# Attention loop: copy, turn, sums and scaling of finished heads placed in other periods

## The chip, the cores and the metric

One core of one Trainium2 chip runs the whole program. The metric is the device time of one launch in microseconds. The engines are TensorE (PE), its weight loads (PEld), VectorE (DVE), ScalarE (ACT), GpSimd (POOL) and SyncE (SP), which issues the DMAs.

## The reference

Two layers of an encoder on 1024 tokens of width 1024 in float32, which lie on a grid of 16 rows by 64 columns. Each layer mixes the tokens in three groups of heads (8 heads of neighbourhood attention, 4 of spatial gating, 4 of a Fourier mix), norms every head, projects, and then applies a SwiGLU network:

```python
for l in range(DEPTH):
    proj = rms_norm(x, norm_mix_g[l]) @ w_in[l]
    q, k, v, z_b, x_c = jnp.split(proj, splits, axis=-1)
    mix_a = neighbourhood_attention(q, k, v, rpb[l])
    mix_b = spatial_gating(z_b, ...)
    mix_c = fourier_mix(x_c)
    mix = head_rms_norm(jnp.concatenate([mix_a, mix_b, mix_c], axis=-1), head_norm_g[l])
    x = x + mix @ w_out[l]
    h = rms_norm(x, norm_ffn_g[l])
    x = x + (jax.nn.silu(h @ w_gate[l]) * (h @ w_up[l])) @ w_down[l]
return rms_norm(x, final_norm_g)
```

In the attention every query sees a window of 8 rows by 16 columns of keys: `softmax(q k^T * scale + bias) v` per head. `head_rms_norm` divides each head's 64 values of a token by the root of their mean square.

## The kernel before, in words

Each engine has its own queue, written out by hand as one Python function per engine (`_(pe)`, `_(dve)`, `_(act)`, `_(pool)`, `_(sp)`), and the engines meet only in semaphores. The order in a queue is the order in which the helpers are called. Products in float32 precision are made of three passes over parts called hi and lo.

The attention of a layer works on eight tiles of 128 queries (`TILES`), each with 264 to 384 keys, and on eight heads per tile, so there are 64 score blocks, t = 8 * tile + head. They go in pairs i = t // 2. From pair 8 on, two pairs make a **period** m (pairs 2m and 2m+1, scores of heads 4m to 4m+3), m = 4 to 15; a tile is two periods, and it begins with an even one. Tiles 2 and 5 (m = 4, 5, 10, 11) have 352 keys, tiles 3 and 4 (m = 6 to 9) have 384, tile 6 has 264 and tile 7 has 288.

For one score block: `scores` (TensorE, L2382), `logits` (VectorE adds the bias and takes the maximum, L1760), `probs` (ScalarE's exponential, with its sum, L1185), `turn_halves` (TensorE turns the probabilities, L2538), `turned_even` and `turned_odd` (the probability copies out of the bank by VectorE, L1797, and ScalarE, L1210), `values` (TensorE multiplies with the values of two heads, L2457, into bank 6). `values` of period m are pairs 2m-2 and 2m-1: the last pair of a tile comes in the even period behind it.

The finished heads of a tile then pass these steps:

- `heads_copy` (VectorE, L1812): copy of bank 6; waits for the tile's last values. The next tile's first values wait for it.
- `turn_heads` (TensorE, L2472): turns them to token-major form in bank 7; waits for the copy and for `tile_raw` of the tile before, which frees the bank.
- `head_square` (ScalarE, L1223).
- `head_sums` (VectorE, L1784): the sums of 64 squares.
- add and power (GpSimd, L875 and L877): the reciprocal root. Ahead of the add stands the square of the exponential sums of the same tile (L872).
- `head_norms` (VectorE, L1817): the scaling, from bank 7 into the place of the squares.
- `turn_tokens` (TensorE, L2479): the turn back into bank 7; waits for the scaling.
- `tile_raw` (ScalarE, L1229): the raw copy of bank 7 into the mixed output.

GpSimd's queue also splits the pieces of the output weights (`piece_lo`, L821): one behind the power of tile 1, two behind that of tile 5, two behind that of tile 6. `probs` of the first head of a tile waits, from the third tile on, for the squared sums (L872) of the tile two before:

```python
if t >= 16 and t % 8 == 0:
    act.wait_ge(o_eps, l * 8 + t // 8 - 1)
```

Behind the loop, `out_early(0)` (three pieces of three passes, L2233 to L2235) begins the output projection; each piece waits for its `piece_lo`. Then come the last turns, heads 6 and 7, and the rest of the projection.

Of the kernel before, what the change touches and what calls it, by code (L numbers as in the profile page):

```python
# [186 lines left out]
def build(nc, x, win, wout, wom, wg, wu, wd, bias, wsp, bsp, lng, lnb, gmix, ghead, gffn, gfin,  # L187
          tw, bd, ident, out):
    ctx = ExitStack()
    with ctx:  # L190
# [317 lines left out]
        def keys(tile):  # L508
            j, rr = TILES[tile]
            return KR[rr] * KC[j]  # L510
# [387 lines left out]
        def _(act):  # L898
# [158 lines left out]
            for l in range(DEPTH):  # L1057
# [122 lines left out]
                def probs(t):  # L1180
                    act.wait_ge(l_made, l * 64 + t + 1)
                    if t >= 16 and t % 8 == 0:
                        act.wait_ge(o_eps, l * 8 + t // 8 - 1)
                    w = keys(t // 8)
                    nc.scalar.activation(L[:, t % 4, 0:w], L[:, t % 4, 0:w], ACT.Exp, scale=-1.0,  # L1185
                                         bias=NM[:, t % 4:t % 4 + 1],
                                         accum_out=SUM[:, (t // 8) % 2, t % 8:t % 8 + 1]).then_inc(p_made, 1)
# [13 lines left out]
                def turned_odd(t):  # L1201
                    act.wait_ge(pt_full, l * 64 + t + 1)
                    if t >= 4:
                        act.wait_ge(pv_done, l * 64 + t - 3)
                    w = chunk_keys(t // 8, 0)
                    if t < 2 * SINGLE:
                        nc.scalar.activation(head_probs(t)[0:w], B[3][0:w, 0:NKEY].rearrange("p (n q) -> p n q", q=P),
                                             ACT.Copy).then_inc(pt_act, 1)
                    else:
                        nc.scalar.activation(half_probs(t // 2, 1)[0:w],  # L1210
                                             B[3][0:w, 0:NKEY].rearrange("p (g q) -> p g q", q=DH),
                                             ACT.Copy).then_inc(pt_act, 1)
# [8 lines left out]
                def head_square(tile):  # L1221
                    act.wait_ge(o_turned, l * 8 + tile + 1)
                    nc.scalar.activation(head_squares(tile),  # L1223
                                         B[TILE_BANK[tile]][:, :].rearrange("p (k q) -> p k q", q=P), ACT.Square,
                                         scale=(DH * EPS) ** -0.5).then_inc(o_sq, 1)

                def tile_raw(tile):
                    act.wait_ge(ot_full, l * 8 + tile + 1)
                    nc.scalar.activation(raw_out(tile),  # L1229
                                         B[TILE_BANK[tile]][:, :].rearrange("p (k r c) -> p k r c", k=NP, c=QC),  # L1230
                                         ACT.Copy).then_inc(raw_made, 1)
# [12 lines left out]
                    for n in {0: (), 1: (0, 1, 2), 7: ()}.get(i, (i + 1,)):  # L1244
                        batch_hi(n)
                for m in range(SINGLE // 2, 16):
                    if m % 2 == 0 and m >= 6:
                        tile_raw((m - 6) // 2)
                    for n in {7: (0,), 15: (2,)}.get(m, ()):
                        piece_hi(l, OUT_P + n)  # L1250
                    probs(4 * m)
                    turned_odd(4 * m - 1)
                    probs(4 * m + 1)
                    if m % 2 == 0 and m >= 4:
                        head_square((m - 4) // 2)
                    probs(4 * m + 2)
                    probs(4 * m + 3)
                    if m == 14:
                        piece_hi(l, OUT_P + 1)
                    turned_odd(4 * m + 1)  # L1260
                tile_raw(5)
                turned_odd(63)
                head_square(6)
# [104 lines left out]
        def _(dve):  # L1368
# [136 lines left out]
            for l in range(DEPTH):  # L1505
# [244 lines left out]
                def logits(t):  # L1750

                    tile, h = divmod(t, 8)
                    dve.wait_ge(s_full, l * 64 + t + 1)
                    if t >= 4:
                        dve.wait_ge(pt_full, l * 64 + turns_done(t - 4))
                    if h % 4 == 0:
                        dve.wait_ge(bias_landed[BIAS_BUF[tile]][h // 4], l * 48 + 16 * BIAS_NTH[tile])
                    dve.sem_inc(dve_passed, 1)

                    nc.vector.tensor_tensor_reduce(  # L1760
                        L[:, t % 4, 0:keys(tile)], score_bank(t // 2, t % 2),
                        BIAS[BIAS_BUF[tile]][:, h // 4, h % 4 * keys(tile):(h % 4 + 1) * keys(tile)], -1.0, 3e38,
                        ALU.add, ALU.min, NM[:, t % 4:t % 4 + 1]).then_inc(l_made, 1)
# [13 lines left out]
                def head_sums(tile):  # L1777

                    dve.wait_ge(o_sq, l * 8 + tile + 1)
                    if tile:  # L1780
                        dve.wait_ge(o_rstd, l * 8 + tile)
                    else:
                        dve.wait_ge(hs_norm, l * 3 + 3)
                    nc.vector.tensor_reduce(SS[:, 0:HA].rearrange("p (k r) -> p k r", k=NP),  # L1784
                                            head_squares(tile).rearrange("p k (r d) -> p k r d", d=DH),
                                            AX_X, ALU.add).then_inc(o_red, 1)

                def turned_even(t):
                    dve.wait_ge(pt_full, l * 64 + t + 1)
                    if t >= 4:  # L1790
                        dve.wait_ge(pv_done, l * 64 + t - 3 + (t >= 2 * SINGLE))
                    w = chunk_keys(t // 8, 0)
                    if t < 2 * SINGLE:
                        nc.vector.tensor_copy(head_probs(t)[0:w], B[2][0:w, 0:NKEY].rearrange("p (n q) -> p n q", q=P))\
                            .then_inc(pt_dve, 1)
                    else:
                        nc.vector.tensor_copy(half_probs(t // 2, 0)[0:w],  # L1797
                                              B[2][0:w, 0:NKEY].rearrange("p (g q) -> p g q", q=DH)).then_inc(pt_dve, 1)
# [9 lines left out]
                def heads_copy(tile):  # L1808
                    dve.wait_ge(pv_done, l * 64 + 8 * tile + 8)
                    if tile:  # L1810
                        dve.wait_ge(o_turned, l * 8 + tile)
                    nc.vector.tensor_copy(OC[:, :, :], B[VALUE_BANK][:, :].rearrange("p (k q) -> p k q", q=P))\  # L1812
                        .then_inc(o_copied, 1)

                def head_norms(tile):
                    dve.wait_ge(o_rstd, l * 8 + tile + 1)
                    nc.vector.scalar_tensor_tensor(  # L1817
                        out=head_squares(tile).rearrange("p k (r d) -> p k r d", d=DH),
                        in0=B[TILE_BANK[tile]][:, :].rearrange("p (k r d) -> p k r d", k=NP, d=DH),
                        scalar=EPS ** -0.5,  # L1820
                        in1=SR[:, 0:HA].rearrange("p (k r a) -> p k r a", k=NP, a=1).to_broadcast([P, NP, 2, DH]),
                        op0=ALU.mult, op1=ALU.mult).then_inc(o_norm, 1)
# [13 lines left out]
                    if 2 <= i < 6:  # L1836
                        query_rest(0, i - 2)
                for m in range(SINGLE // 2, 16):
                    if m % 2:
                        heads_copy((m - 3) // 2)  # L1840
                    logits(4 * m)
                    logits(4 * m + 1)
                    turned_even(4 * m - 2)
                    if m % 2:
                        head_norms((m - 5) // 2)
                    logits(4 * m + 2)
                    logits(4 * m + 3)
                    if m % 2 == 0:
                        head_sums((m - 4) // 2)
                    turned_even(4 * m)  # L1850
                turned_even(62)
                head_sums(6)
                head_norms(6)
# [353 lines left out]
        def _(pe):  # L2207
# [29 lines left out]
            for l in range(DEPTH):  # L2237
# [33 lines left out]
                for i, (k, h) in enumerate(X_ORDER):  # L2271
# [7 lines left out]
                    for b in range(4 * h, 4 * h + 4):  # L2279
                        m = slice(b * P, (b + 1) * P)  # L2280
# [278 lines left out]
                for m in range(SINGLE // 2, 16):  # L2559
                    scores(2 * m)  # L2560
                    scores(2 * m + 1)
                    if 2 * m - 1 < SINGLE:
                        turn_pair(2 * m - 1)
                    else:
                        turn_halves(2 * m - 1)
                    if m % 2 == 0:
                        turn_heads((m - 4) // 2)
                    values(2 * m - 2)
                    values(2 * m - 1)
                    if m % 2:  # L2570
                        turn_tokens((m - 5) // 2)
                    turn_halves(2 * m)
                pe.wait_ge(bt_lo, l * 8 + 8)
                out_early(0)
                turn_halves(31)
                turn_heads(6)
                out_early(1)
# [250 lines left out]
```

## Time and profile before

| | |
|---|---|
| three runs | 2023.27, 2024.71, 2027.75 us (median 2024.71) |
| the profiled execution | 2022.06 us, its span 2020.0 us |
| TensorE busy | 1985.4 us, 98% of the span |
| VectorE, ScalarE, GpSimd busy | 1522.2, 895.4, 217.7 us |
| attention loop (m = 4 to 15) | layer 0: 229.69 to 283.87 us; layer 1: 1226.43 to 1280.60 us |
| TensorE's granted clock | 0.998 of full speed in the mean |

Matmuls are pipelined and the ends of their rows are modelled, so that rows of TensorE overlap; their starts say more than their durations. Idle time is printed in brackets with the engine that ended it; "issue" is time for which nothing is shown. A line of the timeline can stand for several like instructions (x12).

### The profile page before, as it was taken

To read this page: it belongs to the slowest core of one execution; us is meant where nothing else is said; L and a number is where in the kernel's file an instruction comes from. 1 tells how busy PE (TensorE), PEld (TensorE's weight loads), DVE (VectorE), ACT (ScalarE), POOL (GpSimd) and SP (SyncE) were. 2 spreads that over 40 slices of the span, in tenths; PEclk is the share of its full clock that TensorE was granted. 3 is DMA by queue.
4 is the path that set the end of the run, shared out by engine and by line. 5 is a ranking of instruction groups with operands and counts; after the bars stand their busy time and mean duration, and the time that the engine had idled before them with its cause. 6 is when DMAs were issued, how large, how long until landed. Compare 5 with 4: busy or idle time off the path is not lost.

```text
span 2020.0 us, 28668 instructions
## 1 busy us (share of the span) xinstructions
PE 1985.4 (98%) x10444; PEld 1651.2 (82%) x10444; DVE 1522.2 (75%) x2517; ACT 895.4 (44%) x1611; POOL 217.7 (11%) x150
## 2 busy tenths in 40 slices
PE   7999999999999999999999999999999999999998
PEld 7888778888888888888898877788888888888887
DVE  7847864798877777787877478557987777778877
ACT  6453873443333333544544548634333333334443
POOL 1221343100000000000013122530000000000000
PEclk9999999999999999999999999999999999999999
DMA  6965744125333337533378667431343333393333
GB/s 239 219 167 143 219 132 149 48 84 177 131 104 105 105 105 276 182 98 97 117 209 201 159 158 231 148 104 42 130 161 111 105 105 104 105 337 96 100 96 123
DMA packets 130986, 288.88 MB, mean 143 GB/s; under 512 B 12960, under 2 KB 17952, under 8 KB 130592
## 3 DMA queue, kind: packets, MB, share of 16 engines
q1 hardware_dynamic: 105184, 237.78, 36.1%
q0 software_dynamic: 10880, 20.97, 6.2%
q10 hardware_dynamic: 14784, 28.31, 3.9%
q8 instruction: 84, 1.38, 0.3%
q14 instruction: 54, 0.44, 0.1%
HBM read 227.77 MB, written 59.24 MB: 142 GB/s over the span
## 4 chain that ended last, share of the span: by engine, by line
PE 87%; DVE 6%; ACT 3%; issue 3%; ACTq 0%; POOL 0%; DMA 0%; DVEq 0%
PE bank L2233 27%; PE bank L2234 27%; PE bank L2235 27%; PE bank L2457 1%; PE bank L2382 1%; ACT logits L1185 1%; DVE s_lo L1474 1%; PE bank L2538 1%; DVE t_lo L1897 0%; DVE logits L1760 0%; PE bank L2479 0%; PE bank L2345 0%; ACT probs_t L1210 0%; ACT h_hi L915 0%; PE bank L2361 0%
## 5 line engine op out<-in xcount | busy, mean ns | idle before, releaser
L2233 PE MATMUL bank<-t_hi,s_hi 128*128 128x512 f32 (+1 forms) x1336 | 516.9, 387 | 0.7 <-DVE hid_cu L2010 0.4
L2234 PE MATMUL bank<-t_lo,s_hi 128*128 128x512 f32 (+1 forms) x1336 | 516.4, 386 | 0.0
L2235 PE MATMUL bank<-t_hi,s_lo 128*128 128x512 f32 (+1 forms) x1336 | 516.3, 386 | 0.0
L2233 PEld LDWEIGHTS bank<-t_hi,s_hi 128*128 128x128 f32 x1336 | 250.9, 188 | 52.5 <-DVE hid_cu L2010 1.3
L2235 PEld LDWEIGHTS bank<-t_hi,s_lo 128*128 128x128 f32 x1336 | 250.9, 188 | 50.9
L2234 PEld LDWEIGHTS bank<-t_lo,s_hi 128*128 128x128 f32 x1336 | 250.9, 188 | 50.6
L2233 PE MATMUL bank<-b_hi,s_hi 128*128 128x512 f32 x528 | 206.0, 390 | 0.1
L2235 PE MATMUL bank<-b_hi,s_lo 128*128 128x512 f32 x528 | 205.5, 389 | 0.0
L2234 PE MATMUL bank<-b_lo,s_hi 128*128 128x512 f32 x528 | 205.4, 389 | 0.0
L988 ACT ACTIVATE s_hi<-w_u 128x512 fp32r<-128x512 f32 x142 | 89.6, 631 | 232.7 <-PE bank L2235 175.2
L988 ACT ACTIVATE s_hi<-w_down 128x512 fp32r<-128x512 f32 x154 | 97.3, 632 | 198.7 <-PE bank L2235 198.0
L1474 DVE TENSOR_TENSOR s_lo<-w_down,s_hi 128x512 fp32r<-128x512 f32 x154 | 107.4, 698 | 74.0 <-ACT s_hi L988 73.9
L988 ACT ACTIVATE s_hi<-w_g 128x512 fp32r<-128x512 f32 x142 | 89.4, 630 | 162.9 <-PE bank L2235 104.9
L821 POOL TENSOR_TENSOR w_lo<-w_raw,w_hi 128x1024 fp32r<-128x1024 f32 x34 | 84.3, 2493 | 689.1 <-ACT w_hi L928 577.4
L928 ACT ACTIVATE w_hi<-w_raw 128x1024 fp32r<-128x1024 f32 x91 | 93.0, 1053 | 65.9 <-DMA w_raw<-in_win 47.9
L2233 PEld LDWEIGHTS bank<-b_hi,s_hi 128*128 128x128 f32 x528 | 99.1, 188 | 21.4 <-issue 0.9
L2235 PEld LDWEIGHTS bank<-b_hi,s_lo 128*128 128x128 f32 x528 | 99.1, 188 | 20.5
L2234 PEld LDWEIGHTS bank<-b_lo,s_hi 128*128 128x128 f32 x528 | 99.1, 188 | 20.4
L1484 DVE TENSOR_TENSOR t_lo<-t_raw,t_hi 128x512 fp32r<-128x512 f32 x154 | 105.4, 684 | 9.6 <-ACT t_hi L994 9.6
L1474 DVE TENSOR_TENSOR s_lo<-w_g,s_hi 128x512 fp32r<-128x512 f32 x142 | 97.3, 686 | 10.7 <-ACT s_hi L988 10.7
L2233 PE MATMUL bank<-h_hi,w_hi 128*128 128x512 f32 x256 | 101.1, 395 | 0.0
L994 ACT ACTIVATE t_hi<-t_raw 128x512 fp32r<-128x512 f32 x154 | 95.0, 617 | 12.8 <-DMA t_raw<-hidden_b 11.3
(295 smaller groups left out, 3705.8 us busy)
## 6 DMA issues: line engine op xcount, KB each, us to landing
w_raw<-in_win SPq DMA_DIRECT2D x50, 512.0 KB, 5.9
w_g<-in_wg SPq DMA_DIRECT2D x44, 512.0 KB, 3.6
w_u<-in_wu SPq DMA_DIRECT2D x44, 512.0 KB, 4.5
t_raw<-hidden_t SPq DMA_DIRECT2D x88, 256.0 KB, 2.6
w_raw<-in_win POOLq DMA_DIRECT2D x40, 512.0 KB, 6.7
t_raw<-hidden_b SPq DMA_DIRECT2D x66, 256.0 KB, 2.6
hidden_b<-hid_g SPq DMA_DIRECT2D x60, 256.0 KB, 2.0
hidden_t<-hid_x SPq DMA_DIRECT2D x44, 256.0 KB, 2.0
```

The source lines that it names most:

```text
L821: nc.gpsimd.tensor_tensor(WL[s][:, :], WR[s][:, :], WH[s][:, :], ALU.subtract).then_inc(w_ready, 1)
L928: nc.scalar.activation(WH[s][:, :], WR[s][:, :], ACT.Copy).then_inc(w_hi, 1)
L988: nc.scalar.activation(SH[q % W_RING][:, :], weight_block(q), ACT.Copy).then_inc(s_hi, 1)
L994: nc.scalar.activation(TH[t][:, :], TR[t][:, :], ACT.Copy).then_inc(t_hi, 1)
L1185: nc.scalar.activation(L[:, t % 4, 0:w], L[:, t % 4, 0:w], ACT.Exp, scale=-1.0, bias=NM[:, t % 4:t % 4 + 1], accum_out=SUM[:, (t // 8) % 2 ...
L1474: nc.vector.tensor_tensor(SL[q % W_RING][:, :], weight_block(q), SH[q % W_RING][:, :], ALU.subtract)\
L1484: nc.vector.tensor_tensor(TL[t][:, :], TR[t][:, :], TH[t][:, :], ALU.subtract).then_inc(t_lo, 1)
L2233: nc.tensor.matmul(bank, lh, rh, start=start, stop=False, skip_group_check=reopened)
L2234: nc.tensor.matmul(bank, lh, rl, start=False, stop=False, skip_group_check=reopened)
L2235: return nc.tensor.matmul(bank, ll, rh, start=False, stop=stop, skip_group_check=reopened)
L2382: mm = nc.tensor.matmul(score_bank(i, e).rearrange("p (r c) -> p r c", c=KC[j]), qs[hp, c, q0:q0 + P], grid(ks[hp, c, :])[:, 4 * rr:4 * rr ...
L2457: mm = nc.tensor.matmul(B[VALUE_BANK][e * DH:(e + 1) * DH, c * P:(c + 1) * P], VB[j % 2][0:w, rr + n, h * DH:(h + 1) * DH], head_probs(h, ...
```

## The change

Five calls change places, in the loops over m of three queues. Even periods: VectorE scales (tile (m-6)/2) behind the second logits, and copies the heads of the tile just finished at the end, instead of at the start of the odd period; TensorE turns back ahead of the values and turns the heads behind them; ScalarE makes the raw copy behind its second exponential and squares at the end. Odd periods: VectorE makes the sums behind its probability copy. What is left over of tile 5 moves behind the loop. In period 14 `piece_hi` stands behind `turned_odd`.

```diff
@@ ScalarE
                 for m in range(SINGLE // 2, 16):
-                    if m % 2 == 0 and m >= 6:
-                        tile_raw((m - 6) // 2)
                     for n in {7: (0,), 15: (2,)}.get(m, ()):
                         piece_hi(l, OUT_P + n)
                     probs(4 * m)
                     turned_odd(4 * m - 1)
                     probs(4 * m + 1)
-                    if m % 2 == 0 and m >= 4:
-                        head_square((m - 4) // 2)
+                    if m % 2 == 0 and m >= 6:
+                        tile_raw((m - 6) // 2)
                     probs(4 * m + 2)
                     probs(4 * m + 3)
+                    if m % 2 == 0:
+                        head_square((m - 4) // 2)
+                    turned_odd(4 * m + 1)
                     if m == 14:
                         piece_hi(l, OUT_P + 1)
-                    turned_odd(4 * m + 1)
@@ VectorE
                 for m in range(SINGLE // 2, 16):
-                    if m % 2:
-                        heads_copy((m - 3) // 2)
                     logits(4 * m)
                     logits(4 * m + 1)
+                    if m % 2 == 0 and m >= 6:
+                        head_norms((m - 6) // 2)
                     turned_even(4 * m - 2)
                     if m % 2:
-                        head_norms((m - 5) // 2)
+                        head_sums((m - 5) // 2)
                     logits(4 * m + 2)
                     logits(4 * m + 3)
                     if m % 2 == 0:
-                        head_sums((m - 4) // 2)
+                        heads_copy((m - 2) // 2)
                     turned_even(4 * m)
+                head_norms(5)
                 turned_even(62)
@@ TensorE
+                    if m % 2 == 0 and m >= 6:
+                        turn_tokens((m - 6) // 2)
+                    values(2 * m - 2)
+                    values(2 * m - 1)
                     if m % 2 == 0:
                         turn_heads((m - 4) // 2)
-                    values(2 * m - 2)
-                    values(2 * m - 1)
-                    if m % 2:
-                        turn_tokens((m - 5) // 2)
                     turn_halves(2 * m)
                 pe.wait_ge(bt_lo, l * 8 + 8)
                 out_early(0)
+                turn_tokens(5)
                 turn_halves(31)
```

TensorE's queue from the second scores of period 8 to the second turn of period 9, first before, then with the change (L2382, L2538 and so on are L2383, L2539 there, since a line is added above; of the six score rows of a period the last stands here). `att_sq` is turned back, `att_heads` turned.

```order
L2382 MATMUL bank<-k_hi,q_lo 128x384 x2
L2538 MATMUL bank<-ident,logits 128x64 x12
L2472 MATMUL bank<-ident,att_heads 128x128 x4
L2457 MATMUL bank<-probs_t,v_band_90 64x128 x12
L2538 MATMUL bank<-ident,logits 128x64 x12
...
L2538 MATMUL bank<-ident,logits 128x64 x12
L2457 MATMUL bank<-probs_t,v_band_89 64x128 x12
L2479 MATMUL bank<-ident,att_sq 128x128 x4
L2538 MATMUL bank<-ident,logits 128x64 x12
```

```order
L2383 MATMUL bank<-k_hi,q_lo 128x384 x2
L2539 MATMUL bank<-ident,logits 128x64 x12
L2480 MATMUL bank<-ident,att_sq 128x128 x4
L2458 MATMUL bank<-probs_t,v_band_90 64x128 x12
L2473 MATMUL bank<-ident,att_heads 128x128 x4
L2539 MATMUL bank<-ident,logits 128x64 x12
...
L2539 MATMUL bank<-ident,logits 128x64 x12
L2458 MATMUL bank<-probs_t,v_band_89 64x128 x12
L2539 MATMUL bank<-ident,logits 128x64 x12
```

The turn back has gone from the end of the odd period to the front of the values of the even one, and the turning of the heads from ahead of these values to behind them.

VectorE's queue over the even period 8 and the first rows of period 9, before and with the change. `att_heads` is the copy, `head_ss` the sums, `att_sq<-bank,head_rstd` the scaling.

```order
L1760 ISA logits,minus_max<-bank,bias_64 128x384
L1760 ISA minus_max 128x1
L1797 COPY probs_t<-bank 128x6x64
...
L1784 TENSOR_REDUCE head_ss<-att_sq 128x8
L1797 COPY probs_t<-bank 128x6x64
L1812 COPY att_heads<-bank 128x512
L1760 ISA logits,minus_max<-bank,bias_64 128x384
```

```order
L1760 ISA logits,minus_max<-bank,bias_64 128x384
L1760 ISA minus_max 128x1
L1817 SCALAR_TENSOR_TENSOR att_sq<-bank,head_rstd 128x4x128
L1797 COPY probs_t<-bank 128x6x64
...
L1812 COPY att_heads<-bank 128x512
L1797 COPY probs_t<-bank 128x6x64
L1760 ISA logits,minus_max<-bank,bias_64 128x384
```

The scaling stands between the second logits and the probability copy; the copy of the heads is the last but one of the even period; the sums have left it.

## Rows read from the trace of the kernel before

**Rows 1.** Table by stretches: start:end, us, busy us of each engine, PEclk, DMA share, GB/s
```profile
core 0: us, PE busy (x) PEld busy (x) DVE busy (x) ACT busy (x) POOL busy (x), PEclk, DMA share, GB/s
200.00:300.00 100.00, 92.12 (x1086) 74.37 (x1085) 75.11 (x207) 76.52 (x199) 37.73 (x32) 1.00 0.60 182
300.00:400.00 100.00, 100.00 (x464) 83.29 (x463) 60.43 (x81) 41.77 (x63) 29.58 (x13) 1.00 0.29 98
```
**Rows 2.** Timeline of TensorE, periods 8 and 9: start us, duration us, instruction
```profile
247.97 0.43 PE L2382 MATMUL bank<-k_hi,q_hi 64*128 64x384 f32 x2
...
249.14 0.53 PE L2538 MATMUL bank<-ident,logits 64*128 64x64 f32 x12
249.60 0.66 PE L2472 MATMUL bank<-ident,att_heads 128*128 128x128 f32 x4
250.18 1.53 PE L2457 MATMUL bank<-probs_t,v_band 128*64 128x128 f32 x24
251.64 0.59 PE L2538 MATMUL bank<-ident,logits 64*128 64x64 f32 x12
252.04 0.43 PE L2382 MATMUL bank<-k_hi,q_hi 64*128 64x384 f32 x2
...
255.26 0.88 PE L2457 MATMUL bank<-probs_t,v_band 128*64 128x128 f32 x12 [0.45 <-ACT probs_t L1210]
256.06 0.66 PE L2479 MATMUL bank<-ident,att_sq 128*128 128x128 f32 x4
...
257.05 0.41 PE L2382 MATMUL bank<-k_hi,q_hi 64*128 64x352 f32 x2
```
**Rows 3.** Timeline of VectorE, periods 8 and 9, and one row of period 15
```profile
248.97 0.56 DVE L1760 CUSTOM_DVE_ANT_0 logits<-bank,bias 128x384 f32<-128x384 f32 x1 [0.22 <-PE bank L2382]
...
249.94 0.55 DVE L1797 COPY probs_t<-bank 128x384 f32<-128x384 f32 x1
...
251.77 0.69 DVE L1784 TENSOR_REDUCE head_ss<-att_sq 128x8 f32<-128x512 f32 x1 [0.33 <-ACT att_sq L1223]
...
252.84 0.68 DVE L1812 COPY att_heads<-bank 128x512 f32<-128x512 f32 x1
253.44 0.55 DVE L1760 CUSTOM_DVE_ANT_0 logits<-bank,bias 128x384 f32<-128x384 f32 x1
...
254.86 0.68 DVE L1817 SCALAR_TENSOR_TENSOR att_sq<-bank,head_rstd 128x512 f32<-128x512 f32 x1
...
279.73 0.45 DVE L1760 CUSTOM_DVE_ANT_0 logits<-bank,bias 128x288 f32<-128x288 f32 x1
```
**Rows 4.** Timeline of ScalarE, period 8, and its probability copy in period 9
```profile
248.62 0.59 ACT L1229 ACTIVATE att_raw<-bank 128x512 f32<-128x512 f32 x1
249.58 0.61 ACT L1185 ACTIVATE logits<-logits,minus_max 128x384 f32<-128x384 f32 x1 [0.36 <-DVE minus_max L1760]
...
250.19 0.47 ACT L1210 ACTIVATE probs_t<-bank 128x384 f32<-128x384 f32 x1
250.56 0.60 ACT L1185 ACTIVATE logits<-logits,minus_max 128x384 f32<-128x384 f32 x1
...
254.64 0.47 ACT L1210 ACTIVATE probs_t<-bank 128x384 f32<-128x384 f32 x1
```
**Rows 5.** Timeline of GpSimd: the power in period 9, the two pieces in period 15
```profile
252.88 1.64 POOL L877 TENSOR_TENSOR head_rstd<-head_ss,minus_half 128x8 f32<-128x8 f32 x1
...
280.40 4.70 POOL L821 TENSOR_TENSOR w_lo<-w_raw,w_hi 128x1024 fp32r<-128x1024 f32 x2
```
**Rows 6.** Timeline of TensorE: start of period 15, first early product, last turns
```profile
278.05 0.38 PE L2382 MATMUL bank<-k_hi,q_hi 64*128 64x288 f32 x2
...
283.87 0.50 PE L2233 MATMUL bank<-h_hi,w_hi 128*128 128x512 f32 x1
...
286.14 0.54 PE L2538 MATMUL bank<-ident,logits 64*96 64x64 f32 x12
286.61 0.66 PE L2472 MATMUL bank<-ident,att_heads 128*128 128x128 f32 x4
```
**Rows 7.** Table by stretches, columns as in rows 1, two microseconds near the end
```profile
2014.00:2016.00 2.00, 0.40 (x2) 0.11 (x1) 1.56 (x4) 0.00 (x0) 0.00 (x0) 0.50 0.80 263
```

## The prediction

> **What bounds the kernel now.** I read the table by stretches first. TensorE is busy for all of 300 to 400 us but for only 92.12 us of 200 to 300 us [rows 1]: the attention stage is where TensorE waits, and the stage behind it has no gap in which a later start could be made up. So what lengthens or shortens TensorE's attention loop goes to the end one for one. Both layers run the same program, so each term counts twice.
>
> Next the timeline of TensorE over one even and one odd period (m = 8 and 9, 384 keys) [rows 2]. Even, from 247.97 (called T): scores, probabilities turned at T+1.17, heads turned at T+1.63, values at T+2.21, probabilities turned at T+3.67, next period at T+4.07. Odd, from 252.04 (T'): the second head pair's values begin only at T'+3.22, after an idle time that ScalarE's probability copy ended; turn back at T'+4.02, next period at T'+5.01. The two cost 9.08 us. VectorE shows why the odd one is late: it copies the heads at 252.84, ahead of the logits, the first of which thus begins at T'+1.40, where in the even period it begins at T+1.00 [rows 3].
>
> **The even period afterwards.** The turn back now stands ahead of the values and waits for the scaling, which VectorE does behind the first two logits. These cannot begin before T+1.00, since they need this period's scores (the row's idle time is ended by them). The scaling takes the place of the probability copy that began at 249.94, T+1.97, and lasts 0.68 us [rows 3]: done at T+2.65. From a producer's end to TensorE's start I take 0.15 us: ScalarE's probability copy that begins at 254.64 ends at 255.11 [rows 4], and TensorE's values, which waited for it, begin at 255.26 [rows 2]. TensorE has nothing to do from T+1.63 on and stands for about 1.15 us, until T+2.80. From there all is back to back with the pitches of rows 2: turn back 0.59, values 1.46, heads turned 0.58, probabilities turned 0.40: next period at T+5.83. Two waits could be longer and are not. The turning of the heads needs the raw copy of the tile before: ScalarE can start it at T+3.46 (end of the turn back, 0.66 us), its second exponential having begun at T+2.59, and needs 0.59 us [rows 4]; done by T+4.1, needed at T+4.85. The copy of the heads waits for the last values (T+4.9) with the next probability copy queued behind it on VectorE, but that one needs a turn that ends at T+6.0 anyway. An even period goes from 4.07 to 5.83 us, **+1.76**. There are five with a turn back (m = 6, 8, ... 14): +8.8.
>
> **The odd period afterwards.** Copy of heads, scaling and turn back are gone; the sums are added behind the probability copy. The logits begin at T'+1.00 again, so the exponential and ScalarE's probability copy stand as in the even rows: the copy begins at T'+2.22 and lasts 0.47 [rows 4], the second values begin at T'+2.84, take 0.73 (half of 1.46), the turn 0.40: next period at T'+3.97 against 5.01, **-1.04**. The sums (0.69 us) delay only the last two logits, whose exponentials are wanted in the following period at about T+1.2, ahead of its new wait. Five such periods (m = 5, 7, ... 13): -5.2. The first even period (m = 4) only turns the heads behind the values instead of ahead of them: between 0 and 0.58, and 0.1 taken, because the values then wait for ScalarE's probability copy (T+2.84, and they begin at T+2.21 now).
>
> **GpSimd, which the diff does not touch.** Its queue is in program order: add and power per tile, behind tile 1 one piece of the output weights to split, behind tile 5 two, and only then the squared exponential sums of the next tile. The power (1.64 us) begins 0.42 us after the end of the sums (251.77 and 0.69 [rows 3], 252.88 [rows 5]); two pieces take 4.70 us [rows 5]. All of it hangs on the sums, which move from the end of the even period to T'+2.43 of the odd one (1.97 and a copy's pitch of 0.46).
> - Tile 1 (m = 7): sums end at T'+3.1, power 3.5 to 5.2, piece to 7.5, squared sums there at 7.6. The next period begins at 3.97, so this is T+3.65 of m = 8, and ScalarE's first exponential of that tile, which waits for them, began at T+1.61 until now [rows 4]. Behind it the probability copy ends at T+4.8, second values at 4.95, second exponential 4.7, raw copy 5.3 to 5.9, heads turned 5.95, next period at T+6.93: **+1.1** on top of the 1.76.
> - Tile 5 (m = 15, T' = 278.05): today the pieces run from 280.40 to 285.10, T'+7.05 [rows 5], and the early output products, three pieces of 0.76 us each, begin at 283.87, T'+5.82 [rows 6], so that the last piece is just in time. Now the sums end at about T'+2.8 (288 keys: logits of 0.45 instead of 0.55 us [rows 3] and shorter scores, 0.3 less than above), power 3.2 to 4.85, pieces to 7.15 and 9.5. TensorE comes to the products between T'+4 and T'+5, wherever ScalarE lets it, does one, and stands until 7.25 for the second piece and until 9.6 for the third; it is through at T'+10.35 instead of 8.09 (286.14). Then the turn back of tile 5, new at this place, and its raw copy (0.66, 0.59 and 0.1 between) stand ahead of the turning of heads 6: T'+11.7 instead of 8.56 (286.61) [rows 6]: **+3.14**. The later steps of the tail (powers of tiles 6 and 7, more pieces) I cost at nothing: they move by no more than TensorE does, with the early products as cover; without that cover each would cost up to the 2.35 us of a piece.
>
> **Sum.** 8.8 - 5.2 + 0.1 + 1.1 + 3.14 = 7.9 us per layer; for the four tiles of fewer keys, with shorter logits ahead of the new wait, I take off 0.4. 7.5 us twice is 15.0. The profiled execution took 2022.06 us (span 2020.0), which gives 2037.1; the three runs shown have their median at 2024.71, 2.65 above it, and against that I forecast **2039.7 us**, +0.74%. A measurement of this kernel can tell about 0.2% (4 us) from no change.
>
> **A rule against it.** The attention stretch keeps the granted clock at 1.00 with 8 us of idle in it [rows 1]; at the very end, with TensorE busy for 0.40 of 2 us, it is 0.50, which is 1.2 GHz [rows 7]. The change makes two stands of about 1.5 us close together in the early products; whether the clock falls there is a rival below. The Trainium skill, "TensorE: Matmul & The Clock Gate", Part 1, says that an idle array is put on half clock and gets the full one back by activity; by that rule the sum would grow by that rival's price, by the clock in rows 1 it does not.
>
> **The rivals.**
> - *Only TensorE's wait costs.* If the squared sums and the pieces come in time, 1.1 goes, and the 3.14 becomes about 0 (-1.0 in period 15 as in the other odd ones, +0.6 and +0.3 for turn back and raw copy behind the products): 3.3 per layer, 2031.3. For it: no such wait is in the rows today. Against: GpSimd's order and 2.35 us a piece. Chance 0.14.
> - *Faster.* The place is the turn back in the even period, and the end of the scaling decides. If TensorE finds it done at T+1.63, that period is 4.07 + 0.59 = 4.66 and the pair 8.63 instead of 9.08: -0.45 for each of five tiles, and with GpSimd hidden too 2.3 per layer, 2020.1 in all. For it: the late logits of the odd periods do go. Against: VectorE would have to take logits before their scores are there. Chance 0.05.
> - *No change that shows.* The waits come out half as long as I have them, because the edges are smoother than the pitches of two periods say: 2024.7 give or take 4. Chance 0.06.
> - *The clock falls* in the stands of the tail: the early products, 2.27 us at full clock [rows 6], take double, and at most as much again is lost behind them: 2.3 to 4.5 per layer, 2044 to 2049. Chance 0.07.
> - The forecast case keeps 0.68.
>
> **How the numbers follow.** Around the forecast, 0.2 us either way on five even periods and 0.5 on the tail are 1.5 per layer, 3 in all, and the median of a few runs moves by some 2: 2035 to 2045. To leave out no more than 2 in 10 the range takes in the first rival and the lower half of the clock's: 2030.5 to 2047. Faster by over 0.2%: 0.05; within it: 0.06; slower: 0.89.
>
> **What the profile of the changed kernel would show.** A turn back at T+2.8 in even periods, with 1.1 us of idle ended by VectorE's scaling; even periods of 5.8 us (6.9 for m = 8), odd ones of 4.0; GpSimd's two pieces ending near T'+9.5 of period 15, and two stands of 1.5 us inside the first early products. I am wrong if even periods stay below 5 us, if the early products run without a gap, or if TensorE is no longer full from 300 to 400 us.

## The result, and the profile after

The changed kernel takes 2043.18 us in the median of 6 runs (2040.97 to 2043.76), the kernel before 2028.03 us in the 6 runs on the same chips (2023.27 to 2029.96). The ratio is 1.008 with a 95% interval of 1.0069 to 1.0091: 0.8% slower, 14 to 18 us. The profiled execution took 2040.97 us, its span is 2039.0 us against 2020.0.

The forecast was 2039.7 us, +0.74%, against a median of 2024.71 us for the kernel before; the three further runs took 2028.31 to 2029.96 and raised it to 2028.03. The last section shows what the granted clock has to do with that.

The table by stretches first (columns as in [rows 1]); the last two rows are the tail of the attention in layer 1:

```profile
core 0: us, PE busy (x) PEld busy (x) DVE busy (x) ACT busy (x) POOL busy (x), PEclk, DMA share, GB/s
200.00:300.00 100.00, 85.80 (x1047) 67.49 (x1046) 72.36 (x202) 73.50 (x193) 32.27 (x28) 1.00 0.59 178
300.00:400.00 100.00, 100.00 (x467) 83.30 (x466) 57.67 (x77) 40.01 (x60) 34.95 (x18) 1.00 0.31 100
1295.00:1300.00 5.00, 3.07 (x10) 2.19 (x10) 0.00 (x0) 0.00 (x0) 3.00 (x3) 0.72 0.49 196
1300.00:1305.00 5.00, 5.00 (x27) 3.80 (x25) 1.24 (x2) 3.57 (x5) 1.16 (x2) 0.59 0.01 2
```

TensorE is now busy for 85.80 us of the attention stretch instead of 92.12 [rows 1], and still for all of the next one: what is lost is lost in the attention and is not made up. The next rows are TensorE's timeline over an even and an odd period of 384 keys (m = 6 from 238.35, m = 7 from 244.10), the changed kernel's answer to [rows 2]:

```profile
238.35 0.43 PE L2383 MATMUL bank<-k_hi,q_hi 64*128 64x384 f32 x2
...
239.63 0.57 PE L2539 MATMUL bank<-ident,logits 64*128 64x64 f32 x12
241.06 0.65 PE L2480 MATMUL bank<-ident,att_sq 128*128 128x128 f32 x4 [0.85 <-DVE att_sq L1817]
241.64 1.54 PE L2458 MATMUL bank<-probs_t,v_band 128*64 128x128 f32 x24
243.11 0.66 PE L2473 MATMUL bank<-ident,att_heads 128*128 128x128 f32 x4
243.70 0.59 PE L2539 MATMUL bank<-ident,logits 64*128 64x64 f32 x12
244.10 0.43 PE L2383 MATMUL bank<-k_hi,q_hi 64*128 64x384 f32 x2
...
246.92 0.88 PE L2458 MATMUL bank<-probs_t,v_band 128*64 128x128 f32 x12 [0.33 <-ACT probs_t L1210]
247.73 0.59 PE L2539 MATMUL bank<-ident,logits 64*128 64x64 f32 x12
248.12 0.43 PE L2383 MATMUL bank<-k_hi,q_hi 64*128 64x384 f32 x2
```

The turn back begins at T+2.71, after idle time that VectorE's scaling ended; the even period takes 5.75 us and the odd one 4.02. VectorE shows the scaling that TensorE waits for, at T+1.96 as worked out, and the sums in the odd period at T'+2.42:

```profile
239.35 0.56 DVE L1760 CUSTOM_DVE_ANT_0 logits<-bank,bias 128x384 f32<-128x384 f32 x1 [0.21 <-PE bank L2383]
...
240.31 0.69 DVE L1817 SCALAR_TENSOR_TENSOR att_sq<-bank,head_rstd 128x512 f32<-128x512 f32 x1
...
246.52 0.68 DVE L1784 TENSOR_REDUCE head_ss<-att_sq 128x8 f32<-128x512 f32 x1
```

GpSimd's queue for tile 1 (period 7) and for tile 5 (period 15, which begins at 282.92), the counterpart of [rows 5]:

```profile
247.62 1.64 POOL L877 TENSOR_TENSOR head_rstd<-head_ss,minus_half 128x8 f32<-128x8 f32 x1
249.22 2.36 POOL L821 TENSOR_TENSOR w_lo<-w_raw,w_hi 128x1024 fp32r<-128x1024 f32 x1
251.53 0.21 POOL L872 TENSOR_TENSOR exp_sum_sq<-exp_sum 128x8 f32<-128x8 f32 x1
...
286.14 1.64 POOL L877 TENSOR_TENSOR head_rstd<-head_ss,minus_half 128x8 f32<-128x8 f32 x1
287.74 4.67 POOL L821 TENSOR_TENSOR w_lo<-w_raw,w_hi 128x1024 fp32r<-128x1024 f32 x2
```

The squared sums come at 251.53, and ScalarE's first exponential of period 8 (which begins at 248.12) right behind them, at T+3.71:

```profile
251.83 0.62 ACT L1185 ACTIVATE logits<-logits,minus_max 128x384 f32<-128x384 f32 x1 [2.44 <-POOL exp_sum_sq L872]
```

And TensorE at the early products, the answer to [rows 6]: one piece, a stand for the second, a stand for the third, both ended by GpSimd's split:

```profile
287.87 0.50 PE L2234 MATMUL bank<-h_hi,w_hi 128*128 128x512 f32 x1
...
290.16 0.50 PE L2234 MATMUL bank<-h_hi,w_hi 128*128 128x512 f32 x1 [1.32 <-POOL w_lo L821]
...
292.47 0.50 PE L2234 MATMUL bank<-h_hi,w_hi 128*128 128x512 f32 x1 [1.34 <-POOL w_lo L821]
...
293.26 0.60 PE L2480 MATMUL bank<-ident,att_sq 128*128 128x128 f32 x4
293.79 0.54 PE L2539 MATMUL bank<-ident,logits 64*96 64x64 f32 x12
294.64 0.63 PE L2473 MATMUL bank<-ident,att_heads 128*128 128x128 f32 x4 [0.31 <-ACT att_raw L1229]
```

All twelve periods of layer 0, read off the starts of TensorE's scores (for m = 15 up to the first turning of heads behind the loop), in us:

| m | 4 | 5 | 6 | 7 | 8 | 9 | 10 | 11 | 12 | 13 | 14 | 15 |
|---|---|---|---|---|---|---|---|---|---|---|---|---|
| before | 4.26 | 4.84 | 4.05 | 5.13 | 4.07 | 5.01 | 3.95 | 4.91 | 3.76 | 4.63 | 3.75 | 8.56 |
| after | 4.52 | 3.91 | 5.75 | 4.02 | 6.97 | 4.03 | 5.61 | 3.92 | 5.27 | 3.65 | 5.35 | 11.72 |

The sums are 56.92 and 64.72 us: +7.80 us in layer 0, where the forecast had +7.5 per layer. Layer 1 has the same lengths up to m = 14 within 0.01 us; its m = 15 is 13.02, because the granted clock falls there (0.72 and 0.59 in the table above). So the change itself accounts for twice 7.80 = 15.6 us. The other 3.4 us of the 19.0 between the two profiled spans are 0.2 ahead of the loop of layer 0, 0.7 between the loops (clock 0.72 at 1220 to 1225 us), 1.3 in period 15 of layer 1 and 1.2 behind it.

### The profile page after: what moved, and what is told of

It reads as the page before. It is cut to its first block, busy times and chain, and to the rows that moved or that the text cites. A ratio compares the mean times of both kernels' runs of the same rounds, so it can differ in the third digit from the quotient of the medians.

```text
span 2039.0 us, 28668 instructions
## 1 busy us (share of the span) xinstructions
PE 1991.9 (98%) x10444; PEld 1653.5 (81%) x10444; DVE 1522.5 (75%) x2517; ACT 897.2 (44%) x1611; POOL 217.2 (11%) x150
## 4 chain that ended last, share of the span: by engine, by line
PE 87%; DVE 6%; issue 3%; ACT 2%; POOL 1%; ACTq 0%; DMA 0%; DVEq 0%; POOLq 0%
PE bank L2234 27%; PE bank L2236 27%; PE bank L2235 27%; PE bank L2458 2%; PE bank L2383 1%; DVE s_lo L1474 1%; DVE t_lo L1898 0%; PE bank L2473 0%; PE bank L2480 0%; POOL w_lo L821 0%; DVE logits L1760 0%; PE bank L2438 0%; PE bank L2346 0%; PE bank L2539 0%; ACT h_hi L915 0%
## 5 line engine op out<-in xcount | busy, mean ns | idle before, releaser
L1474 DVE TENSOR_TENSOR s_lo<-w_g,s_hi 128x512 fp32r<-128x512 f32 x142 | 97.3, 685 | 10.7 <-ACT s_hi L988 10.7
L2235 PE MATMUL bank<-h_lo,w_hi 128*128 128x512 f32 x256 | 100.3, 392 | 0.0
```

The lines of the kernel that those rows point to most:

```text
L1474: nc.vector.tensor_tensor(SL[q % W_RING][:, :], weight_block(q), SH[q % W_RING][:, :], ALU.subtract)\
L2235: nc.tensor.matmul(bank, lh, rl, start=False, stop=False, skip_group_check=reopened)
```

## The experiments

Period lengths are read as in the table above; where nothing else is said they are those of layer 0.

**1. The turn back behind the values.**

```diff
 TensorE, changed kernel
-                    if m % 2 == 0 and m >= 6:
-                        turn_tokens((m - 6) // 2)
                     values(2 * m - 2)
                     values(2 * m - 1)
+                    if m % 2 == 0 and m >= 6:
+                        turn_tokens((m - 6) // 2)
```

> The changed kernel, with TensorE's turn back behind the values of the same even period instead of ahead of them (heads turned right behind it). Theory (the chain logits, scaling, turn back, raw copy, turning of heads all lies in one period): the idle time ahead of the turn back goes, but a wait for the raw copy appears ahead of the turning of the heads. Second values wait for VectorE's probability copy, now behind the scaling (T+3.12 and 0.15), so 3.27 to 4.0; turn back to 4.6; raw copy 4.7 to 5.3; heads turned from 5.45; next period at T+6.4 with 384 keys, against 5.75 in the changed kernel: five periods of +0.65 and two layers, about 6 us slower than the changed kernel. Rival (only the place of the turn back ahead of the values costs): the 1.1 us of idle go, even periods of 4.6 to 4.7 us, 11 us faster than the changed kernel. A second rival would be no difference: the wait is the same wherever it stands.

One run: 2054.37 us, against 2040.47 for a run of the changed kernel beside it. Period 6, with 384 keys, takes 6.36 us (expected 6.4; 5.75 in the changed kernel), the even periods with fewer keys 6.24, 5.89 and 5.97. Period 8, where the late exponential adds to it and the clock falls as well, takes 8.67. TensorE in period 6, which begins at 238.52:

```profile
240.31 0.88 PE L2458 MATMUL bank<-probs_t,v_band 128*64 128x128 f32 x12
241.69 0.88 PE L2458 MATMUL bank<-probs_t,v_band 128*64 128x128 f32 x12 [0.49 <-DVE probs_t L1797]
242.49 0.66 PE L2480 MATMUL bank<-ident,att_sq 128*128 128x128 f32 x4
243.93 0.63 PE L2473 MATMUL bank<-ident,att_heads 128*128 128x128 f32 x4 [0.78 <-ACT att_raw L1229]
```

The wait for the scaling is gone, and two others stand in its place: 0.49 us for the probability copy, which VectorE makes behind the scaling, and 0.78 us for the raw copy that frees bank 7. The place of the turn back is not what costs; that scaling, turn back, raw copy and turning of heads follow one another inside one period is. The rival falls, with the one of no difference. The price was expected too small, 3.25 us per layer: the twelve periods sum to 70.74 us against 64.72, because periods 7 and 9 (4.22 and 4.56), 8 and 15 (12.83) grow too. A part of this is clock, 0.66 at 255 to 260 us and 0.50 at 295 to 300, so that periods 6, 10, 12 and 14 carry the reading and the total does not.

**2 and 3. GpSimd's pieces elsewhere in its queue.** First the piece of tile 1 alone, then the two of tile 5 as well:

```diff
 GpSimd, changed kernel
                     nc.gpsimd.tensor_tensor(S2[:, :], SUM[:, t % 2, :], SUM[:, t % 2, :], ALU.mult).then_inc(o_eps, 1)
+                    for n in {2: (0,), 5: (1, 2)}.get(t, ()):
+                        piece_lo(l, OUT_P + n)
                     pool.wait_ge(o_eps, l * 8 + t + 1)
...
-                    for n in {1: (0,), 5: (1, 2), 6: (3, 4)}.get(t, ()):
+                    for n in {6: (3, 4)}.get(t, ()):
```

> The changed kernel, with GpSimd's splitting of the first output piece behind the squared exponential sums of tile 2 instead of ahead of them. Theory (period 8 is long because ScalarE's exponential waits for these sums behind the piece): period 8 goes from 6.97 to about 5.8 us, nothing else changes: 1.15 us per layer, 2.3 in all. Rival (period 8 is long for another reason, such as its keys or the first use of a buffer): it stays at 6.97.

One run, 2039.61 us. Period 8 takes 5.74 us in both layers instead of 6.97; every other period up to m = 14 is as in the changed kernel within 0.01 us. ScalarE's first exponential of period 8 (which begins at 250.43) is released by VectorE again, at T+1.60:

```profile
252.03 0.61 ACT L1187 ACTIVATE logits<-logits,minus_max 128x384 f32<-128x384 f32 x1 [0.33 <-DVE minus_max L1762]
```

That is -1.23 us per layer for the piece, as the theory has it.

> The kernel of the run before, with the two pieces of tile 5 split ahead of its add and power instead of behind them. Theory (the stands in the early products are GpSimd's pieces, late because they hang on the sums): ScalarE's hi parts are there at about T'+1.7 and 2.7 of period 15, the pieces run from there to 6.4, the early products are through near T'+7.2 instead of 10.3; but the power of tile 5 then runs 6.7 to 8.4, and TensorE waits for the scaling ahead of the turn back of tile 5: heads of tile 6 turned at about T'+10.7 instead of 11.7. So about 1.0 us per layer from this and 1.15 from the run before, 4.3 us in all against the changed kernel, and without the two long stands close together the granted clock should stay at 1.00 in both tails. Rival (the tail is late because of the turn back and raw copy standing there): the early products run through but heads of tile 6 are turned at 11.5 or later. Second rival (the clock, not the stands, carries the tail of layer 1): no difference in layer 0.

2038.54 us in the median of 5 runs, ratio to the kernel before 1.0049 (1.0033 to 1.0065), against 1.008 for the changed kernel. In both layers the heads of tile 6 are turned at T'+10.56 (expected 10.7, 11.72 before the edit). TensorE in that tail, period 15 beginning at 284.29; the stands between the products are gone, and one for the scaling has come, since GpSimd makes the power of tile 5 (291.00 to 292.64) only behind the pieces:

```profile
290.49 0.40 PE L2238 MATMUL bank<-h_hi,w_lo 128*128 128x512 f32 x1
...
293.42 0.66 PE L2482 MATMUL bank<-ident,att_sq 128*128 128x128 f32 x4 [1.63 <-DVE att_sq L1819]
```

The gain of the two edits in the periods is 64.72 - 62.30 = 2.4 us per layer. The part of the expectation on the clock is wrong: it falls to 0.66 at 295 to 300 us in this run, behind the 1.63 us stand, and to 0.79 at 1300 to 1305 us in layer 1.

**4. The changed kernel again.**

> The changed kernel once more, to see which parts of its profile repeat. Theory: period lengths of the loop in both layers within 0.05 us of 4.52, 3.91, 5.75, 4.02, 6.97, 4.03, 5.61, 3.92, 5.27, 3.65, 5.35, 4.95. The granted clock below 1.00 near 1230 us and behind the tail of layer 1 is a matter of when in the execution a stand falls: it may be absent, or at the tail of layer 0 instead, and the span moves by 1 to 2.5 us with it. Rival (the clock always falls behind the tail's stands of layer 1, and they cost what the sum lacks): the same stretches at the same clock.

One run: 2040.47 us, span 2038.5. All period lengths repeat within 0.03 us in both layers, but for m = 15 of layer 1, which takes 12.56 us instead of 13.02. The clock falls behind the tail of layer 1 again (0.93 and 0.73 at 1295 to 1305 us); it falls near 215 us in layer 0, where it had not, and not near 1220 us, where it had. So neither theory has it whole: the place near the start of the attention changes from run to run, the tail of layer 1 came twice out of two.

**5. The copy of the heads alone.**

```diff
 VectorE, kernel before
-                    if m % 2:
-                        heads_copy((m - 3) // 2)
                     logits(4 * m)
...
                     if m % 2 == 0:
                         head_sums((m - 4) // 2)
+                        heads_copy((m - 2) // 2)
                     turned_even(4 * m)
```

> The kernel before, with only the copy of the heads moved: from the start of the odd period to the end of the even one, behind the sums and ahead of the probability copy. Theory (VectorE's odd periods are late because sums, probability copy and copy of heads, 1.7 us together, all come behind waits that end at T+3.8 of the even period, in whatever order): the copy runs T+4.4 to 5.1, the probability copy behind it, the logits still begin at T'+1.4; odd periods stay at 5.0 (384 keys) and even ones at 4.1, the span within 0.5 us of the kernel before apart from the granted clock. So the gain of the odd periods in the changed kernel needs sums and scaling gone, not the copy moved. Rival (the place of the copy ahead of the logits is what costs): odd periods of 4.0 to 4.6 us, 5 to 10 us faster than before.

One run, 2030.3 us. Periods 4 to 14 are 4.26, 4.63, 4.16, 5.03, 4.06, 5.01, 3.97, 4.90, 3.75, 4.54 and 3.75 us: against the kernel before, period 5 is 0.2 us shorter, the rest moves by 0.1 at most, and the sum of the eleven is 0.3 us less. VectorE around the start of period 9 at 255.69: the logits begin at T'+1.40, as in the kernel before [rows 3].

```profile
255.43 0.69 DVE L1784 TENSOR_REDUCE head_ss<-att_sq 128x8 f32<-128x512 f32 x1 [0.33 <-ACT att_sq L1223]
256.03 0.68 DVE L1812 COPY att_heads<-bank 128x512 f32<-128x512 f32 x1
256.63 0.55 DVE L1797 COPY probs_t<-bank 128x384 f32<-128x384 f32 x1
257.09 0.55 DVE L1760 CUSTOM_DVE_ANT_0 logits<-bank,bias 128x384 f32<-128x384 f32 x1
```

What delays VectorE is the work behind the wait for ScalarE's square, in whatever order; moving the copy alone is worth next to nothing. (Period 15 came out 1.5 us longer in both layers, and that is the clock. TensorE's two stands in it, 1.04 us up to T'+2.07 and 0.54 up to T'+3.96, are the same in the kernel before. Behind them the granted clock is 0.66 at 285 to 290 us and at 1285 to 1290 us, where the kernel before has 1.00.)

**6. The scaling ahead of the logits.**

```diff
 VectorE, changed kernel
+                    if m % 2 == 0 and m >= 6:
+                        head_norms((m - 6) // 2)
                     logits(4 * m)
                     logits(4 * m + 1)
-                    if m % 2 == 0 and m >= 6:
-                        head_norms((m - 6) // 2)
```

> The changed kernel, with the scaling ahead of the first two logits of the even period instead of behind them. Theory: the power of GpSimd is done at T+1.15, so the scaling runs 1.2 to 1.9, TensorE turns back at T+2.0 instead of 2.8; but the logits begin at 1.8 instead of 1.0, the exponentials at 2.4, ScalarE's probability copy ends at 3.5, the second values begin at 3.65, the raw copy is done at 4.6, heads are turned at 4.75: next period at T+5.7, as in the changed kernel (5.75). The wait changes its place and not its length. Rival (only the wait for the scaling counts): 0.8 us less per even period, 4.95, 8 us in all.

One run, 2042.86 us. Period 6 takes 5.62 us instead of 5.75, but period 7 then 4.23 instead of 4.02. Period 8 is 0.2 us shorter, and the pairs m = 10, 11 and 12, 13 are 0.1 us shorter or the same. (Period 15 takes 12.84 us instead of 11.72, with the clock at 0.50 at 290 to 295 us.) TensorE in period 6, which begins at 238.69:

```profile
240.60 0.66 PE L2480 MATMUL bank<-ident,att_sq 128*128 128x128 f32 x4
...
242.28 0.88 PE L2458 MATMUL bank<-probs_t,v_band 128*64 128x128 f32 x12 [0.22 <-ACT probs_t L1210]
243.36 0.63 PE L2473 MATMUL bank<-ident,att_heads 128*128 128x128 f32 x4 [0.20 <-ACT att_raw L1229]
```

The turn back begins at T+1.91 instead of 2.71, and 0.8 us earlier buys 0.13 in this period and nothing in the pair: the values and the raw copy are late instead. The rival (4.95 us) falls.

**7. The copy on ScalarE, in the kernel before.** ScalarE makes the copy of the heads in periods 5, 9, 11 and 13:

```diff
 ScalarE
+                def heads_copy_act(tile):
+                    act.wait_ge(pv_done, l * 64 + 8 * tile + 8)
+                    act.wait_ge(o_turned, l * 8 + tile)
+                    nc.scalar.activation(OC[:, :, :], B[VALUE_BANK][:, :].rearrange("p (k q) -> p k q", q=P),
+                                         ACT.Copy).then_inc(o_copied, 1)
+
                 for m in range(SINGLE // 2, 16):
+                    if m in (5, 9, 11, 13):
+                        heads_copy_act((m - 3) // 2)
 VectorE
-                    if m % 2:
+                    if m in (7, 15):
                         heads_copy((m - 3) // 2)
```

> The kernel before, with the copy of the heads of tiles 1, 3, 4 and 5 made by ScalarE behind its first probability copy of the odd periods 5, 9, 11 and 13, where it waits for VectorE's logits, instead of by VectorE ahead of these logits (periods 7 and 15 stay, since ScalarE splits weight pieces there). Theory (what the change gained in the odd periods is VectorE's lateness at the logits, and it can be had without moving the turn back): logits at T'+1.0 instead of 1.4, copy 1.15 to 1.75, exponential at 1.65, second values at 2.9 instead of 3.2; odd periods of 4.45, 4.6, 4.5 and 4.2 us instead of 4.84, 5.01, 4.91 and 4.63, even ones as before: 1.6 us per layer, 3.2 in all, 0.16% faster than the kernel before, at the edge of what the timing can tell. Rival (TensorE then waits for the copy ahead of the first values, or ScalarE falls behind): the odd periods stay within 0.1 us of before, or grow.

2023.25 us in the median of 12 runs, ratio 0.9982 (0.9971 to 0.9992). The four periods take 4.50, 4.66, 4.53 and 4.17 us, all others as before; 55.42 instead of 56.92 us for the twelve, in both layers. ScalarE in period 9, which begins at 254.36:

```profile
255.15 0.47 ACT L1210 ACTIVATE probs_t<-bank 128x384 f32<-128x384 f32 x1
255.52 0.58 ACT L1249 ACTIVATE att_heads<-bank 128x512 f32<-128x512 f32 x1
256.00 0.61 ACT L1185 ACTIVATE logits<-logits,minus_max 128x384 f32<-128x384 f32 x1
```

The copy lies where ScalarE waited for the logits (0.72 us in the kernel before), and the exponential begins at T'+1.64. By the periods this version beats both kernels: 1.5 us per layer, 3.0 us in all. The interval lies wholly below 1, and its middle gives 3.7 us. The timing alone would be weak evidence: ten of the 17 runs of the kernel before beside it took 2028.00 to 2029.51 us at a lower granted clock, and beside runs 8 and 9 the median of that kernel was 2024.57.

**8. The order in period 14.** The change also put ScalarE's second weight piece behind the probability copy there:

```diff
 ScalarE, kernel before
-                    if m == 14:
-                        piece_hi(l, OUT_P + 1)
                     turned_odd(4 * m + 1)
+                    if m == 14:
+                        piece_hi(l, OUT_P + 1)
```

> The kernel before, with the one part of the change that concerns ScalarE's weight pieces alone: in period 14 the hi part of the second output piece is made behind the probability copy instead of ahead of it. Theory: the 1.04 us stand of TensorE ahead of its first turn in period 15 goes, and the early products begin at about T'+5.3 instead of 5.82; but GpSimd's pieces end at T'+7.05 as before (they hang on the power of tile 5), so the third product begins at 7.15 instead of 7.32, and the heads of tile 6 are turned at about T'+8.4 instead of 8.57: 0.15 us per layer is all that is left. Rival (ScalarE's split is what makes period 15 long): 8.0 or less, 1 us and more in both layers.

One run, 2029.08 us. In layer 1, where the clock is 1.00 in these periods, the early products begin at T'+5.82 and the heads of tile 6 are turned at 8.54: nothing is gained. My working had the exponential of period 15 move forward with the copy, but it stands behind both pieces in either order, so that the stand only moves from the first turn to the second values. It is 1.48 us there in both layers. In layer 0 (period 15 from 281.57) the clock falls behind it:

```profile
285.52 1.55 PE L2457 MATMUL bank<-probs_t,v_band 96*64 96x128 f32 x12 [1.48 <-ACT probs_t L1210]
287.00 1.12 PE L2479 MATMUL bank<-ident,att_sq 128*128 128x128 f32 x4
```

```profile
core 0: us, PE busy (x) PEld busy (x) DVE busy (x) ACT busy (x) POOL busy (x), PEclk, DMA share, GB/s
285.00:290.00 5.00, 4.48 (x31) 3.51 (x32) 1.08 (x5) 2.91 (x10) 3.75 (x3) 0.55 0.68 231
```

**9. Both.**

> The kernel with ScalarE's copy of the heads in periods 5, 9, 11 and 13, and this part besides. Theory: the two add up, 1.5 us per layer from the copies and 0.15 from the order in period 14, 3.3 us in all against the kernel before at the same granted clock, 0.16%; the stand of 1.04 us in period 15 is gone, so the clock has one place less to fall at. Rival (they share a limit): period lengths as in the run with the copies alone and the heads of tile 6 turned at 8.57 still.

2024.22 us in the median of 12 runs, ratio 0.9992 (0.9981 to 1.0003). Layer 0 has 55.42 us for the twelve periods, exactly as the copies alone have; layer 1 has 58.49, with the clock at 0.71 and 0.61 in 1275 to 1285 us, at the stand that the new order makes. In layer 0 the same stand, 1.49 us, left the clock at 1.00, and in run 5 the clock fell in this tail with the old order, so that nothing here shows the new order to be the worse one. The two do not add up; the second shows no gain, and I would leave it out.

## Why the prediction was right

- **The even period**, +1.76 us: measured +1.70, 1.66, 1.51 and 1.60 in periods 6, 10, 12 and 14. The wait for the scaling is there, with 0.85 us of idle on the matmul's row; the forecast's 1.15 counts from the start that the pitch allows, the row from the end of the turns. The scaling ended where it was worked out, at T+2.65, and TensorE began 0.06 us behind it instead of 0.15. Runs 1 and 6 show that the wait can be pushed to another place and not away.
- **The odd period**, -1.04: measured -0.93, -1.11, -0.98, -0.99 and -0.98. Of this, 0.59 is the turn back itself, which now lies in the even period. Run 5 shows that the copy's place has next to no part in the rest. Run 7, which takes the copy off VectorE, gains 0.33 to 0.46 us per period.
- **Period 4**, +0.1 taken of 0 to 0.58: measured +0.26.
- **Tile 1's piece**, +1.1: run 2 gives it back with 1.23.
- **The tail**, +3.14: measured +3.16, with a stand for each of the two pieces; run 3 removes them, and then the power of tile 5 is what comes next, as the order of GpSimd's queue says.
- **The sum**, 7.5 per layer: 7.80. The five even periods gave 8.14 (without the piece) where 8.8 - 0.4 was taken, the odd ones -4.99 for -5.2, period 4 0.26 for 0.1, the piece 1.23 for 1.1. So the even periods are 0.3 below the forecast and the other parts 0.5 above, and the sum is closer than its parts. The steps behind the turning of heads 6, costed at nothing, did cost nothing in layer 0: 6.29 us up to the turning of heads 7, against 6.33.
- **The rivals.** That only TensorE's wait costs is excluded by runs 2 and 3; a gain, by the 5.75 us of period 6; no change that shows, by the interval of 14 to 18 us. The clock was given 0.07 as a rival to the forecast, but it is not one or the other: it fell in the tail of layer 1 on top of the forecast sum, +1.3 us up to the turning of heads 6 and another 1.3 up to heads 7 (7.62 us against 6.29 in layer 0).
- **Luck.** The medians differ by 15.15 us, almost the forecast 15.0, but the two profiled executions by 19.0. Both medians hold losses that the sum left out, and these happen to be about equal: 2028.03 lies 6.0 us above the profiled 2022.06, and 2043.18 lies 5.5 above 2022.06 + 15.6. The level of the kernel before, which I took from three runs, also moved by 3.3 us.

## What to carry to other kernels

When steps of a chain are moved between periods, write down for each period the whole chain that now lies inside it; here four steps on three engines came to stand one behind the other, and each swap inside the period only renamed the wait. Follow a moved step also to engines that the edit does not name: GpSimd's queue had weight pieces behind sums that now end at T'+3.1 of the odd period instead of T'+0.42, and moving these pieces alone gave back 2.4 of the 7.8 us. And where one engine is late and another waits for it at the same spot, as ScalarE did here for the logits, a step can be given to the waiting one with nothing else moved.

## What the runs showed of the hardware

The times of the kernel before lie in two groups. Of the 17 runs taken beside runs 8 and 9, nine took 2022.05 to 2024.57 us, at a mean granted clock of 0.997 to 0.999, and eight 2027.9 to 2031.64, at 0.992 to 0.995. The profiled execution is of the first group and has the full clock throughout the attention. In other profiles the clock falls near the start of the attention, where TensorE stands for 1.34 and 1.09 us in a row. These are the two stands in the kernel before, where it does not fall:

```profile
214.43 0.63 PE L2498 MATMUL bank<-ident,xc_tok 128*128 128x128 f32 x4 [1.34 <-DVE h_lo L1804]
216.15 0.40 PE L2382 MATMUL bank<-k_hi,q_hi 64*128 64x288 f32 x2 [1.09 <-DVE minus_max L1760]
```

There the same program goes either way, as the two profiles of the changed kernel show. With the copies on ScalarE the same stands, 1.34 and 1.09 us, end at 215.01 and 216.73. There it fell, in both layers, and the stretches of layer 0 read:

```profile
core 0: us, PE busy (x) PEld busy (x) DVE busy (x) ACT busy (x) POOL busy (x), PEclk, DMA share, GB/s
213.00:218.00 5.00, 2.57 (x18) 1.83 (x18) 4.28 (x8) 4.24 (x9) 4.79 (x3) 0.87 0.02 8
218.00:223.00 5.00, 5.00 (x34) 4.05 (x34) 4.00 (x10) 3.94 (x9) 0.55 (x1) 0.50 0.48 132
```

0.50 is 1.2 GHz, and TensorE was busy for 2.57 of the 5 us in which the clock began to fall. From the end of the second stand to period 4 it is 15.61 us (216.73 to 232.34), against 13.54 in the kernel before (216.15 to 229.69): a price of 2.1 us, and of 0.6 to 2.1 over all the profiles in which it fell here. At the other place, period 15 in run 8, the price is 11.60 against 8.54 us, 3.1 us. The Trainium skill, "TensorE: Matmul & The Clock Gate", Part 1, says that idleness puts the array on half clock, and that the number of slow matmuls at the start of one kernel varies from run to run. The trace agrees with the first, with these numbers, though TensorE was idle only in part where the clock fell; it shows the second at stands in the middle of a kernel. That the slower group of the kernel before is made of such executions fits the sizes and the mean clocks, but no profile of one was taken, so it stays open. Whatever decides in one execution whether the clock falls is not shown either.
